# Staggering the start addresses of split weight slots in on-chip memory: a two-block transformer kernel on one Trainium2 core

## The reference: what is computed

```python
def first_block(x, ...):
    h = _rms_norm(x, attn_norm)
    x = x + _hybrid_mixer(h, w_in, ..., w_out)      # 8 forgetting heads, 8 sparse heads (compressed, selected, window)
    h = _rms_norm(x, ffn_norm)
    return x + _swiglu(h, w_gate, w_up, w_down)     # width 5632

def second_block(x, c, ...):
    mod = silu(c) @ ada_w + ada_b                   # 2048 x 12288, for one vector c
    sh1, sc1, g1, sh2, sc2, g2 = split(mod, 6)
    h = rms_norm(x, mix_pre_g) * (1 + sc1) + sh1
    x = x + g1 * rms_norm(hybrid_mixer(h, w_in, conv..., w_out), mix_post_g)   # 8 heads and a 31-tap convolution
    h = rms_norm(x, ffn_pre_g) * (1 + sc2) + sh2
    return x + g2 * rms_norm((silu(h @ w_gate) * (h @ w_up)) @ w_down, ffn_post_g)
```

## Time and profile before

| | |
|---|---|
| time, median of 2 runs | 2246.19 us (2246.17 to 2246.22) |
| span of the profiled execution, first to last instruction | 2244.4 us |
| outside the span (median less span; the profiled execution has no time of its own) | 1.8 us |
| instructions | 29,239, of them 10,168 matmuls |
| TensorE busy | 99% of the span |
| mean granted TensorE clock | 0.998 of full speed |
| weights and inputs read from HBM | 508 MB, 227 GB/s over the span |

### The profile page before, as it was taken

One profiled execution on the slowest core, in us unless ns is written; L12 is line 12 of the kernel. 1 busy time (PEld: TensorE's weight loads), 2 busy tenths in 40 slices (PEclk: granted clock), 3 DMA queues, 4 the chain that ended last, 5 costly groups with the idle time before them and its releaser, 6 DMA issues.

```text
span 2244.4 us, 29239 instructions
## 1 busy us (share of the span) xinstructions
PE 2219.3 (99%) x10168; PEld 1835.7 (82%) x10168; DVE 1570.4 (70%) x2028; ACT 1094.4 (49%) x1535; POOL 230.8 (10%) x214
## 2 busy tenths in 40 slices
PE   8999999999999999999999999999999999999998
PEld 7888878888888888888888887788888888888886
DVE  6546678877787778877866888997777444454555
ACT  5556574544434444344455776654443444444443
POOL 4003001000000000000001886000010000000000
PEclk9999999999999999999999999999999999999999
DMA  7666627888888888888856664767887666666664
GB/s 233 184 183 179 206 76 273 273 294 283 283 283 295 288 278 285 287 289 281 272 164 192 193 182 122 276 231 249 284 282 249 191 192 191 188 190 194 190 187 148
DMA packets 274500, 511.74 MB, mean 228 GB/s; under 512 B 20071, under 2 KB 28949, under 8 KB 274124
## 3 DMA queue, kind: packets, MB, share of 16 engines
q1 hardware_dynamic: 270252, 509.94, 72.1%
q10 hardware_dynamic: 4128, 0.26, 0.1%
HBM read 508.04 MB, written 2.10 MB: 227 GB/s over the span
## 4 chain that ended last, share of the span: by engine, by line
PE 95%; DVE 2%; ACT 1%; issue 1%; DMA 0%; SPq 0%; DVEq 0%; ACTq 0%
PE bank L1072 32%; PE bank L1088 29%; PE bank L1089 29%; PE bank L1043 1%; PE bank L1140 1%; PE bank L1057 1%; PE bank L1173 0%; PE bank L1161 0%; ACT prob_mid L1583 0%; DVE w_both L2075 0%; PE bank L911 0%; ACT w_both L1545 0%; DMA raw<-in_w_out 0%; PE bank L1179 0%; PE bank L1207 0%
## 5 line engine op out<-in xcount | busy, mean ns | idle before, releaser
L2075 DVE TENSOR_TENSOR w_both<-raw,w_both 128x1024 fp32r<-128x1024 f32 x764 | 950.0, 1247 | 530.9 <-ACT w_both L1545 519.1
L1545 ACT ACTIVATE w_both<-raw 128x1024 fp32r<-128x1024 f32 x764 | 807.4, 1060 | 968.3 <-PE bank L1072 907.7
L1088 PE MATMUL bank<-w_both,act_hi 128*128 128x512 f32 x1984 | 777.1, 392 | 0.0
L1089 PE MATMUL bank<-w_both,act_lo 128*128 128x512 f32 x1984 | 773.3, 390 | 0.0
L1072 PE MATMUL bank<-w_both,act_hi 128*128 128x512 f32 x2176 | 582.0, 391 | 0.9 <-issue 0.5
L1072 PEld LDWEIGHTS bank<-w_both,act_hi 128*128 128x128 f32 x2176 | 407.8, 188 | 86.8 <-issue 0.9
L1088 PEld LDWEIGHTS bank<-w_both,act_hi 128*128 128x128 f32 x1984 | 372.9, 188 | 76.4 <-issue 0.2
L1089 PEld LDWEIGHTS bank<-w_both,act_lo 128*128 128x128 f32 x1984 | 372.9, 188 | 76.1
L1088 PE MATMUL bank<-w_both,mid_hi 128*128 128x512 f32 x960 | 375.8, 391 | 1.4 <-ACT w_both L1545 0.6
L1089 PE MATMUL bank<-w_both,mid_lo 128*128 128x512 f32 x960 | 373.7, 389 | 0.0
L2033 DVE SCALAR_TENSOR_TENSOR ada_acc<-ada_raw,c_act,ada_acc 128x512 f32<-128x512 f32 x360 | 269.7, 749 | 12.9 <-DMA ada_raw<-in_ada_w 5.8
(11 more groups left out here) (313 smaller groups left out, 1000.6 us busy)
## 6 DMA issues: line engine op xcount, KB each, us to landing
ada_raw<-in_ada_w SPq DMA_DIRECT2D x192, 512.0 KB, 5.1
raw<-in_w_gate SPq DMA_DIRECT2D x176, 512.0 KB, 4.3
raw<-in_w_up SPq DMA_DIRECT2D x176, 512.0 KB, 4.2
raw<-in_w_down SPq DMA_DIRECT2D x176, 512.0 KB, 4.4
raw<-in_w_in SPq DMA_DIRECT2D x168, 512.0 KB, 3.7
raw<-in_w_out SPq DMA_DIRECT2D x60, 512.0 KB, 5.4
raw<-in_cmp_w_k SPq DMA_DIRECT2D x4, 512.0 KB, 4.8
raw<-in_cmp_w_v SPq DMA_DIRECT2D x4, 512.0 KB, 4.3
```

The lines of the kernel that those rows point to most:

```text
L1088: pe.matmul(A_[t][:, :], h_, w_hi[:, s, kk, :], start=(k == 0), stop=False)
L1089: pe.matmul(A_[t][:, :], l_, w_hi[:, s, kk, :], start=False, stop=False)
L1545: act.activation(w_hi[:, U % SPLIT_SLOTS].rearrange("p k n -> p (k n)"), raw_of(c, u).rearrange("p k n -> p (k n)"), ACT.Copy).then_inc(hi ...
L2075: dve.tensor_tensor(w_lo[:, U % SPLIT_SLOTS].rearrange("p k n -> p (k n)"), raw_of(c, u).rearrange("p k n -> p (k n)"), w_hi[:, U % SPLIT_ ...
```

## The change

It changes places in memory and nothing else. `mid_step`, 64 bytes, is put ahead of mid_lo. Each of the eight slots of w_both gets 64 bytes behind it, which no instruction touches, so that the slots are 4,160 bytes apart instead of 4,096. The last filler of the left end gives up 128 bytes, so that the longest chain of tiles still ends ahead of act_lo. The views w_hi and w_lo have the same shapes as before.

```diff
         LINE = 512
+        STEP = 16
...
         mid_hi = sb("mid_hi", [P, KD, T], F32R)
+        filler("mid_step", 4 * STEP)
         mid_lo = sb("mid_lo", [P, KD, T], F32R)
         raw = sb("raw", [P, RAW_SLOTS, KPU, CW])
-        w_both = sb("w_both", [P, 2, SPLIT_SLOTS, KPU, CW], F32R)
+        w_both = sb("w_both", [P, 2, SPLIT_SLOTS, KPU * CW + STEP], F32R)[:, :, :, 0:KPU * CW].rearrange(
+            "p a s (k n) -> p a s k n", k=KPU)
         w_hi, w_lo = w_both[:, 0], w_both[:, 1]
...
-        filler("fill_small", 416 - 4 * TT * (D // CW))
+        filler("fill_small", 416 - 8 * STEP - 4 * TT * (D // CW))
```

## The result

The changed kernel takes 2286.25 us (median of 2 runs, 2285.49 to 2287.01) against 2246.19: a ratio of 1.0175, 95% interval 1.013 to 1.022. It is slower by 40 us, outside the range of 2238 to 2260, and inside the band of 2% that I had called no change. Its profiled execution has a span of 2283.8 us, 39.4 more than before.

The account below looks back on a forecast made before the run. TensorE was taken as the bound: 9,120 split-product matmuls at 226.7 ns, 2,067 us, plus 177 us for the rest and 1.8 us outside the span gave 2246.2, stated as 2246.5 us; range 2238 to 2260 us.

Parts of the forecast that it names:

- What bounds the kernel, and the instructions: TensorE's 226.7 ns start-to-start distance over 9,120 split-product matmuls bounds; no instruction or wait changes, so no term there.
- The fixed 177 us: Everything outside the split products (transposes, attention, stage changes, the ends): 177 us of the 2,244.4 us span.
- The moving operand: Split-product matmuls reading w_both slots at eight new places: taken as nought, between 91 us gained and 43 us lost.
- The lower bound: Best case for the split products' moving operand: a loss of 24 cycles per matmul goes away, 91 us gained.
- The stationary operand: Only mid_lo moves, by 64 bytes, in 960 weight loads: nought, with bounds a tenth of the moving operand's.
- The split instructions and the loads: VectorE and ScalarE splits stay within 3% of 1.25 and 1.06 us; loads into raw and ada_raw cost nought.
- Rival C: Loads into raw touch five 512-byte blocks instead of four, lengthening packets: 70 us slower, 2316 us; chance 0.03.
- A: In split products, weight load and moving stream conflict at equal places within 512 bytes; 80 us gained, 2166 us; chance 0.07.
- B: Place changes within each split-product unit lose the settled 226.7 ns: 231.4 ns, 43 us slower, 2289 us; chance 0.08.
- The rule that was weighed: Skill's warm matmul spacing, 215.8 ns for 512 columns; were layout the whole difference, the kernel would take 2147 us.

Follow-up runs that it names:

- TensorE alone: No kernel computation: each layout's places replayed as 96 matmuls, no other engine or DMA working; before 226.7 ns, changed 231.1 with act and 232.1 with mid.
- the groups by themselves: No kernel computation: groups of 48 matmuls, only TensorE running, operand places or sizes varied by group; 226.7 ns at place 0, 233.1 at 192.

## Why the prediction was wrong

**What bounds the kernel, and the instructions.** Right: TensorE's distance from start to start is the only term, and it is the one that moved. The fixed 177 us stayed fixed as far as the rows tell: the two stretches give 42 us on the 9,120 matmuls, within 3 of the span's 39.4.

**The moving operand: the step that failed.** I took nought, between a gain of 91 us and a loss of 43. The first reason was that 226.7 ns is the same for high and low slots, for act and for mid. That was true and said nothing: in all these the moving and the stationary operand stood at the same place within 256 bytes, since every tile began at a multiple of 512. A quantity that never varies in a trace can't be shown harmless by it. The second reason, that the stream passes all places four times whatever it begins at, was an argument without a row, and the runs with constant places contradict it: 229, 232 and 233 ns for 64, 128 and 192. The third, that every start stays at a multiple of 64, fitted the number 32 and no more; at a multiple of 64 it can still cost 6.6 ns. What was right there: writes into neighbouring slots cost nothing, as TensorE alone shows.

The lower bound was misread too. It took the transposes' 110 ns for two cycles on each of 128 columns and 8 over, and from this 24 cycles to be gained at 512. In the groups by themselves 128 moving columns took 5.31 us for 48 (at 405.24), 110.6 ns, and 256 columns 5.76 us, 120.0 ns. So 110 ns at 128 columns is no price per column, and the gain of 91 us had no ground; no fp32r group of 512 columns came below 226.7 ns.

The term's real size: the mean over the changed kernel's four differences, from the groups by themselves, is (229.0 + 232.5 + 233.1 + 226.7) / 4 = 230.3 ns, 3.6 above before, 9,120 x 3.6 = 33 us. Settling and mid_lo make up the other 6 or so: the products with act have 231.0 ns, 0.7 above that mean, and those with mid, where the stationary operand changes its place at every other matmul as well, 232.1. With these prices the four lengths, in the order of the rows, would be 2.75, 2.74, 2.78 and 2.80 us (an estimate; that the first runs from slot 2 to slot 3 is counted from the trace), against 2.77, 2.75, 2.78 and 2.79.

**The stationary operand.** I called it a tenth of the same bounds, at most. mid_lo and raw together cost 6.5 us on their own, against that tenth's 4.5 us at the loss's bound: too small an allowance, since the price was too low. Against slots at 0 a stationary operand at 64 stands at the dear difference, 233.1 ns: 6.4 ns on each of 960 matmuls, and not 4.7. The prices give (8 x 226.7 + 4 x 233.1) / 12 = 228.8 ns for these units, and the kernel has 229.0.

**The split instructions and the loads.** Right: 1,247 to 1,244 ns and 1,060 to 1,059, inside the 3%; DMA at 0.86 and 279 GB/s, following TensorE. Rival C is excluded by the layout with everything at 64.

**The rivals.** A had the right object, the relation of the two reads, and the wrong sign: before, all matmuls stood at the best difference that was tried. B had the right side and nearly the right size (43 us for 40), and its sign, longer distances in the middle of all stages, came true with means of 231 and 232 ns. Its mechanism holds in part: low slots at 64 show settling at 3.7 ns. But its largest step, the 256 bytes between w_hi and w_lo, is free, and constant places carry most of the loss (33 of 39.4 us). That its 43 us came so near is partly luck. I gave it 0.08 for the reason that slots and rows change all the time without a trace, and they did so by multiples of 512 only.

**The range.** The bounds of the unknown cost were -91 and +43 us, and I cut the range at +14. Where a trace has no row at all for a term of 9,120 instances, nought is one value among others; the range should have gone to the bound.

**The rule that was weighed.** The Trainium skill (TensorE: Matmul & The Clock Gate, Back-to-back issue gap) gives N / 2.4 + 2.5 ns, 215.8 ns for 512 columns. In bfloat16 the measured 215.8 ns agree. For fp32r neither 226.7 nor what places add is in it. The Trainium skill (SBUF — State Buffer, Who interferes with whom), in a passage which I had not weighed, has TensorE's two read ports, for the moving operand and for the weight load, as independent. For fp32r the runs show that the two reads are not independent in time, whatever the ports are: with TensorE alone at work, moving only the stationary operand by 64 bytes takes the distance from 226.7 to 233.1 ns.

**What stays open.** What in the memory has the period of 256 bytes, which weight load the moving stream meets, why both operands at 4 are slow though their difference is 0, why changing between 0 and 64 costs and going round four places does not, and where the 32 cycles at the best place go. The runs show prices, not the circuit.

## What to carry to other kernels

With fp32r operands on TensorE, let the moving and the stationary tile begin at the same place modulo 256 bytes, itself a multiple of 32, for every pair that meets, and step both by multiples of 256: in these runs that was the best difference tried, and the worst multiple of 64 cost 3% of the stream. A difference that changes within the stream can cost as well (between 0 and 64 it did, between 0 and 256 not), so padding slots apart to avoid conflicts can create them. And when a trace has only one value of a quantity, it bounds nothing about the others; a few groups of matmuls by themselves in one profile gave the table here.

## What the runs showed of the hardware that I had not expected

- The distance of fp32r matmuls (512 columns, granted clock 1.00) depends, at multiples of 64 bytes, on moving place less stationary place modulo 256: 226.7 ns at 0, 229.0 at 64, 232.5 at 128, 233.1 at 192. With the moving operand 4 bytes off it was 236.7. In bfloat16 it was 215.8 at the places tried.
- After a change of that difference the distances took up to eleven matmuls to settle, and in some groups none. In the whole kernel two changes of 64 bytes in each 12 matmuls cost 3.7 ns a matmul, two of 256 nothing.
- Narrower stationary operands didn't help with 512 moving columns (230.0 and 231.7 ns with 64 and 32, against 226.7 with 128), but did with 256 (113.5 ns with 64, 120.0 with 128).
- VectorE and ScalarE did not respond to the new places: their splits took 1,244 to 1,250 and 1,059 to 1,062 ns in all kernels. The loads of w_gate landed in 4.4 to 4.6 us, against 4.3 before, with raw at 64 as with raw at 0.
